# Where the causal mask joins the attention scores: from a TensorE identity matmul to a VectorE add in PSUM

## The reference

```python
def masked_softmax(s, mask):
    p = jax.nn.softmax(jnp.where(mask, s, NEG_BIG), axis=-1)
    return jnp.where(mask, p, 0.0)

        s = (jnp.einsum('bqhd,bkhd->bhqk', qn, k_nope).astype(jnp.float32)
             + jnp.einsum('bqhd,bkd->bhqk', qr, k_rope).astype(jnp.float32)) * scale
        qpos = q0 + jnp.arange(Q_BLOCK)
        p = masked_softmax(s, kpos[None, :] <= qpos[:, None])
...
    x = layer_norm(DEEPNORM_ALPHA * x + mixed, ln1_g, ln1_b)
    x = layer_norm(DEEPNORM_ALPHA * x + peer(x, peer_w_query, peer_sub_keys, peer_u, peer_v), ln2_g, ln2_b)
```

## Time and profile before

| | us |
|---|---|
| median of 3 runs | 2108.43 |
| lowest, highest | 2106.35, 2108.76 |
| the profiled execution's own time | 2107.81 |
| its span in the profile | 2106.1 |
| TensorE busy in the span | 2041.2 |
| VectorE busy | 1495.8 |
| ScalarE busy | 1187.7 |

### The profile page before, as it was taken

One profiled execution on the slowest core, in us unless ns is written; L12 is line 12 of the kernel. 1 busy time (PEld: TensorE's weight loads), 2 busy tenths in 40 slices (PEclk: granted clock), 3 DMA queues, 4 the chain that ended last, 5 costly groups with the idle time before them and its releaser, 6 DMA issues.

```text
span 2106.1 us, 36550 instructions
## 1 busy us (share of the span) xinstructions
PE 2041.2 (97%) x11636; PEld 1744.8 (83%) x11636; DVE 1495.8 (71%) x2958; ACT 1187.7 (56%) x2023; POOL 715.4 (34%) x646
## 2 busy tenths in 40 slices
PE   8999999999999999999999999999999999999997
PEld 6987888888887888788788888888888878888886
DVE  6666768888888655655676567788888886555556
ACT  4456457766657644545444554567755685554443
POOL 1100005877874311111120000088787561111111
PEclk9999999999999999999999999999999999999999
DMA  5654546777773467667565734477777615766664
GB/s 187 205 181 132 178 151 180 188 182 189 189 183 103 134 215 226 209 223 227 178 200 169 228 114 153 166 181 189 187 183 189 186 59 182 218 221 219 226 221 144
DMA packets 179781, 384.12 MB, mean 182 GB/s; under 512 B 52528, under 2 KB 85328, under 8 KB 179696
## 3 DMA queue, kind: packets, MB, share of 16 engines
q1 hardware_dynamic: 139632, 372.26, 54.4%
q0 software_dynamic: 40064, 10.81, 6.3%
HBM read 365.04 MB, written 17.96 MB: 182 GB/s over the span
## 4 chain that ended last, share of the span: by engine, by line
PE 86%; DVE 5%; DMA 4%; ACT 2%; issue 1%; POOL 0%; SPq 0%; POOLq 0%; DVEq 0%; ACTq 0%
PE wide L1689 35%; PE acc L1675 9%; PE wide L1675 9%; PE acc L1676 5%; PE wide L1676 5%; PE acc L1663 3%; PE acc L1664 3%; PE acc L1665 3%; PE acc L2171 3%; DMA raw<-in_front 2%; PE acc L1678 1%; PE wide L1678 1%; ACT hi L680 1%; DMA gt<-table 1%; PE tr L1867 1%
## 5 line engine op out<-in xcount | busy, mean ns | idle before, releaser
L680 ACT ACTIVATE hi<-raw 128x1024 fp32r<-128x1024 f32 (+1 forms) x644 | 676.1, 1050 | 641.8 <-DMA raw<-in_peer_v 335.1
L1029 DVE TENSOR_TENSOR lo<-raw,hi 128x1024 fp32r<-128x1024 f32 x520 | 635.4, 1222 | 388.0 <-ACT hi L680 386.6
L623 POOL DMA_INDIRECT table<-picks,spots x256 | 478.7, 1870 | 263.5 <-DVE spots L1499 138.6
L1675 PE MATMUL acc<-xT,hi 128*128 128x512 f32 x896 | 321.8, 398 | 0.0
L1689 PE MATMUL wide<-hi,w_lo 128*128 128x512 f32 x1016 | 314.1, 390 | 7.3 <-DVE w_lo L1603 7.0
L1675 PE MATMUL wide<-xT,hi 128*128 128x512 f32 x868 | 311.8, 398 | 4.3 <-DVE lo L1029 4.2
L1689 PE MATMUL wide<-lo,w_hi 128*128 128x512 f32 x1016 | 313.1, 389 | 0.0
L656 POOL TENSOR_TENSOR big<-big,gt 128x128 f32 x248 | 119.5, 482 | 569.8 <-DMA gt<-table 558.0
L1689 PE MATMUL wide<-hi,w_hi 128*128 128x512 f32 x1016 | 313.1, 389 | 0.0
L1676 PE MATMUL acc<-xT,lo 128*128 128x256 f32 x1024 | 266.5, 281 | 0.0
L1676 PE MATMUL wide<-xT,lo 128*128 128x256 f32 x992 | 258.2, 281 | 0.0
(11 more groups left out here) (330 smaller groups left out, 3032.9 us busy)
## 6 DMA issues: line engine op xcount, KB each, us to landing
raw<-in_peer_u SPq DMA_DIRECT2D x256, 512.0 KB, 3.5
raw<-in_peer_v SPq DMA_DIRECT2D x254, 512.0 KB, 4.4
raw<-in_front SPq DMA_DIRECT2D x114, 512.0 KB, 3.7
table<-blank SPq DMA_DIRECT2D x16, 1024.0 KB, 7.5
gt<-table SPq DMA_DIRECT2D x254, 64.0 KB, 4.1
ln_par<-in_ln POOLq DMA_DIRECT2D x10, 512.0 KB, 5.9
raw<-in_front SPq DMA_DIRECT2D x12, 384.0 KB, 3.1
w<-in_cmp_w POOLq DMA_DIRECT2D x16, 256.0 KB, 4.2
```

Source lines behind the costliest of these rows:

```text
L623: pool.indirect_dma_start(table[l], bass.IndirectOffsetOnAxis(spots[:, u, k:k + 1], 0), picks[:, 2, 0, u * TOPK + k:u * TOPK + k + 1], Non ...
L680: nc.scalar.activation(hi[:, s, :width], raw[:, s, :width], ACT.Identity).then_inc(hi_done, 1)
L1029: nc.vector.tensor_tensor(lo[:, s], raw[:, s], hi[:, s].bitcast(F32), ALU.subtract).then_inc(lo_done, 1)
L1675: mm(bank, hi[:, s, c], xT[:, :, k], start=k == 0, stop=False)
```

## The change

TensorE no longer adds the mask. The score matmuls end their PSUM groups themselves, and in `largest(u)` VectorE adds `causal` in place onto the own key blocks of the unit's four heads (128x4x128 in PSUM, with the mask broadcast over the heads), waits for that, and takes the maxima as before. `DVE_STEPS` counts the linked instructions of a layer: 12 more.

```diff
@@ -1325,6 +1325,8 @@
                     keys_n = (unit(u)[2] + 1) * P
                     dve.wait_ge(wide_ready, l * NU + u + 1)
+                    own_block = wide[:, u % 2].rearrange("p (h k) -> p h k", h=4)[:, :, keys_n - P:keys_n]
+                    st.link(nc.vector.tensor_tensor(own_block, own_block, causal[:].unsqueeze(1).broadcast_to([P, 4, P]), ALU.add))
                     nc.vector.tensor_reduce(negmax[:, u % 2], wide[:, u % 2].rearrange("p (h k) -> p h k", h=4)[:, :, :keys_n],
                                             AX.X, ALU.max, negate=True).then_inc(max_ready, 1)
@@ -1946,26 +1948,19 @@
                     banks = wide[:, u % 2].rearrange("p (b h k) -> p b h k", b=2, h=2)
-                    def masked(b):
-                        return mm(banks[:, b, :, keys_n - P:keys_n], ident_r[:], causal_r[:].unsqueeze(1).broadcast_to([P, 2, P]),
-                                  start=False, stop=True, skip_group_check=True)
-
                     if kind == "mla":
                         for b in range(2):
                             for h in range(2):
-                                mm(banks[:, b, h, :keys_n], qT[:QKD, 4 * hg + 2 * b + h, tok], kT[:QKD, 4 * hg + 2 * b + h, :keys_n],
-                                   start=h == 0, stop=False, skip_group_check=True)
-                            ins = masked(b)
+                                ins = mm(banks[:, b, h, :keys_n], qT[:QKD, 4 * hg + 2 * b + h, tok], kT[:QKD, 4 * hg + 2 * b + h, :keys_n],
+                                         start=h == 0, stop=h == 1, skip_group_check=True)
...
                                 half = slice(b * HD, b * HD + HD)
-                                mm(banks[:, b, h, :keys_n], nqT[half, 2 * hg + h, tok],
-                                   nkT[half, (0 if kind == "sel" else GROUPS) + hg, :keys_n],
-                                   start=h == 0, stop=False, skip_group_check=True)
-                        for b in range(2):
-                            ins = masked(b)
+                                ins = mm(banks[:, b, h, :keys_n], nqT[half, 2 * hg + h, tok],
+                                         nkT[half, (0 if kind == "sel" else GROUPS) + hg, :keys_n],
+                                         start=h == 0, stop=h == 1, skip_group_check=True)
                     ins.then_inc(wide_ready, 1)
...
-DVE_STEPS = 74
+DVE_STEPS = 86
```

## The result

The change made the kernel slower: 2114.19 us median of 9 runs (2110.37 to 2117.31) against 2108.13 of before (9 runs beside it, 2105.76 to 2111.14). The ratio is 1.0030, 95% interval 1.0021 to 1.0039. The prediction said 2109.8 with no measurable change at 78%. 2114.19 is barely inside its range, which ended at 2114.3, but the ratio lies clear of the 0.2% within which the prediction would not tell a change from none, and the case that came true, a fall of TensorE's clock, had been given one chance in ten.

What follows compares the result with a forecast made beforehand. TensorE, busy 97%, was taken to bound the kernel, with VectorE leading at the attention's ends. Per layer 0.72 + 2.16 - 1.9 = +1.0 us, both +2.0 on 2107.81, giving 2109.8; range 2107.0 to 2114.3.

Steps and rivals of the forecast that it cites:

- a fall of TensorE's clock: Rival, attention's tail: thinner TensorE work halves the clock, 1.7 to 3.5 us a layer, +5.4 to +9.0 in all; chance 10%.
- the add's time: VectorE's mask add, 128x512 float32 in PSUM: about 0.72 us linked, at least 0.60, at most 1.26.
- unit 0's add: Start of the attention: the add delays the exponentials that scores(2) waits for, costing TensorE 0.72 us a layer.
- adds of units 1 to 8: Middle of the attention: VectorE's idle time and unit 0's exponentials cover these adds, so they cost nothing.
- saving of a unit where TensorE leads: scores(3) to scores(9): dropping two mask matmuls saves 0.24 to 0.34 us a unit, 1.9 a layer.
- adds of units 9 to 11, less unit 9's mask: Attention's tail, led by VectorE: three adds at full price, 2.16 us a layer; +1.9 with unit 9's saved mask.
- the sum with the clock full: Attention, per layer: 0.72 + 2.16 - 1.9 = +1.0 us; both layers +2.0.
- the clock in the tail: TensorE's granted clock at the attention's end was expected to stay at 1.00; a fall had 10%.
- the wash: Main forecast, whole kernel: a small loss of +0.4 to +3.0 us, inside the 0.2% bound; chance 74%.
- the dear write: Rival, VectorE's add: writing the PSUM bank it reads takes 1.26 us, +6.3 in all, 2114.1; chance 8%.
- The hidden tail: Rival: adds hidden everywhere, including units 9 to 11, every mask pair counts, 5.8 to 8.2 us faster; chance 4%.
- Another stage shifts by chance: Rival, outside the changed stretch: a tile's arrival or the half clock's place moves, up to 5 us either way; 4%.

Runs made afterwards that it cites:

- experiment 2: Changed kernel with the masks of units 9, 10 and 11 back on TensorE, units 0 to 8 on VectorE: 2107.77 us, ratio 1.0002 to the kernel before.
- experiment 3: Changed kernel with the masks of units 0 and 9 to 11 back on TensorE, units 1 to 8 on VectorE: 2107.81 us, ratio 1.0004 to before.
- experiment 4: Changed kernel with the masks of units 0 to 8 back on TensorE, only units 9 to 11 on VectorE: 2114.44 us, ratio 1.0032 to before.
- experiment 1: Changed kernel plus 4, 9 and 6 identity matmuls ahead of TensorE's waits for the weights of units 8, 9 and 10: 2108.85 us, ratio 1.0006.
- experiment 10: Changed kernel with only the longest tail gap filled, 9 identity matmuls ahead of unit 9's transposes: 2111.76 us, ratio 1.0014 to before.
- experiment 6: Changed kernel with all three tail gaps filled, plus 7 identity matmuls ahead of the routing stage's eighth tile: 2108.56 us, ratio 1.0005 to before.
- experiment 7: Changed kernel with masks of units 0 and 9 to 11 back on TensorE, plus 7 identity matmuls in the routing stage: 2103.66 us, ratio 0.9985.
- experiment 11: Changed kernel, masks of units 0 and 9 to 11 on TensorE, routing gap filled, plus 5 and 4 identity matmuls in the tail gaps: 2103.49 us, ratio 0.9983.
- 12: Repeat of the kernel with masks of units 0 and 9 to 11 on TensorE and the routing gap filled, tail unfilled: 2103.67 us, ratio 0.9989.

## Why the prediction was wrong

| step | forecast, us a layer | measured |
|---|---|---|
| the add's time | 0.72 linked | 0.71 to 0.73 (149.36 to 150.07, 157.76 to 158.49) |
| unit 0's add | +0.72 | +0.72 (experiment 2 less 3) |
| adds of units 1 to 8 | 0 | none shown: the saving beside them comes out whole |
| saving of a unit where TensorE leads | 0.24 to 0.34 | 0.27 (experiment 3, six units) |
| adds of units 9 to 11, less unit 9's mask | +1.9 | +1.8 (experiment 4, layer 0) |
| the sum with the clock full | +1.0 | +0.9 (experiment 1) |
| the clock in the tail | full (falls: 1 in 10) | falls, +1.7 and +1.5 |

The working of the sum was right as far as it went. The step that failed is the term that it left out: "A layer: 0.72 + 2.16 - 1.9 = +1.0 us" takes TensorE's clock at 1.00 in the tail, and the fall stands only as a rival with 10% beside 74% for the wash. The runs showed the fall in both layers of both profiles of the changed kernel, at +1.7 and +1.5 us (experiment 1). The second term put at nothing was everything outside the attention; there the profiles show a further fall in layer 0's routing stage, below. The rival had its mechanism, its place, its side and its size: the prediction put it at +5.4 to +9.0, and +6.1 was measured, though not all of that is the tail's. It had even reckoned that the worst 5 us would hold about 2.6 us of work; they hold 2.77, where the thin row of before has 3.07.

What it lacked was the step from there to a chance. Of the six tails that carry all the adds unfilled or with one gap filled (two profiles of the changed kernel, one of experiment 10) five fell; with the three gaps filled none of four did. None of the rows it gives shows a stretch as thin as 2.6 of 5 us at full clock. But the trace of before does hold such stretches, so no rule on how thin is too thin comes out of it: busy 2.79 of 5 us from 1040.5 and 2.49 from 2082.5, both with the granted clock at 1.00 in them and for over 10 us behind them, and experiment 4's layer 0 adds another. One row also stood further from the tail in the prediction than it is: the matmuls before the fall at 1173 were of a few columns only from 1171.0 on, and of 256 before. With one fall and several thin stretches without one to go by, even odds would have been fair, and 10% was not; that the measured time still lies inside the stated range is luck, since the range reached so far for the sake of the dear write, which did not happen.

The fall costs as little as the lower end of the forecast's 1.7 to 3.5 a layer, since part of the 7 us at half clock would have been spent waiting for VectorE anyway: the wait ahead of unit 10's transposes shrank to 0.24 us (1.59 at full clock in experiment 10's layer 1), while the work before it took nearly twice as long.

The rest of the 6.1 us (4.4 to 8.2 by the interval): 1.8 from the two sums, 3.2 from the two falls, and about 1 outside the attention. The fall in the routing stage stands in the profiles of the changed kernel and of five of its variants without that filling (experiments 1 to 4 and 10), and in neither of the two of before. From `y_mla` to the third unit of the routing the changed kernel takes 1.4 us longer than before in layer 0 and 0.6 less in layer 1; with 5.0 in the attention, 0.3 ahead of it and 0.4 between the layers that is the whole 6.5 of the spans. So in this pair of profiles the remainder is that stretch, and experiment 6 shows that filling its gap takes the excess away; the whole times of experiments 1 and 6 don't settle its size. Why the fall comes in the variants and not in the kernel before, though TensorE waits there 1.8 us before and 1.8 to 2.1 in them, is open. So is how much of experiment 7's gain over experiment 3 (4.4 us against their own runs of before) is this fall: filling the same gap in the kernel before gained nothing, and in their profiles the stretch is 0.7 us (layer 0) and 1.8 us (layer 1) shorter in experiment 7.

The other rivals: the dear PSUM write is refuted by the 698 ns. The hidden tail is refuted by experiments 2 to 4. "Another stage shifts by chance" is partly what the routing stage shows, though as both profiles of the changed kernel have its fall and neither of before does, chance is not the word for it. The Trainium skill's sentence on semaphores (VectorE: DVE Perf Modes, The DRAIN you can't avoid), that one after each instruction costs nothing over one after the last, disagrees with the trace again: add to reduction, linked, 0.71 us for an instruction of 0.68; reduction to add, unlinked, 0.61 for one of 0.69 (150.07, then the next add at 150.68).

## What to carry to other kernels

Work taken off TensorE at a place where it already waits can cost time: the idle time grows, and behind it the clock may fall to half for the next microseconds of real work. These traces give no busy time above which that can't happen, so when a change thins a stretch in which TensorE already waits, take the fall as a main case, and read the granted clock of every run, not of one profile. The gap can be filled with dummy matmuls into a bank that is about to be overwritten: here that gave back 1.6 us a layer (experiment 1), and where there was no fall to prevent it cost under 0.1 us (experiment 11).

Split a move by place. The same edit lost at both ends of the attention, where VectorE set the pace, and gained 1.6 us a layer in the middle, where TensorE did. Doing it for units 1 to 8 alone (with the routing gap filled) turned +6 us into -3.4; without the filling the version was not told from the kernel before (+1.0).

## What was unexpected of the hardware

The half-clock stretches of the changed kernel's tails came at the same places in both profiles, at 202 to 208 and at 1246 to 1253. That doesn't hold of every kernel: two profiles of one version (experiments 7 and 12) have a fall in layer 1's tail in the one and none in the other, and in experiment 4, behind the same gaps of 1.10 and 2.24 us, layer 0 kept the full clock and layer 1 did not. A VectorE add that reads and writes the same PSUM bank takes 698 ns, beside 686 for one that writes SBUF.
